# Seventeen tiles of a decoder layer transposed by DMA instead of on TensorE, with modulation in SBUF, earlier residual loads, and the last FFN1 tile normalised in other memory

## The reference

```python
# adaLN: (LayerNorm without affine) * (1 + scale) + shift; shift, scale, gate come from c
h = modulate(x, sh1, sc1)
y = swiglu(h, ffn1_w_gate[l], ffn1_w_up[l], ffn1_w_down[l])
x = layer_norm(ALPHA * x + 0.5 * g1[:, None, :] * y, ln1_g[l], ln1_b[l])
h = modulate(x, sh2, sc2)
y = token_mix(h, w_in[l], attn_sinks[l], pool_w_mix[l], pool_scale[l], w_out[l])
x = layer_norm(ALPHA * x + g2[:, None, :] * y, ln2_g[l], ln2_b[l])
h = modulate(x, sh3, sc3)
y = swiglu(h, ffn2_w_gate[l], ffn2_w_up[l], ffn2_w_down[l])
x = layer_norm(ALPHA * x + 0.5 * g3[:, None, :] * y, ln3_g[l], ln3_b[l])
```

## Time and profile before

| | |
|---|---|
| profiled execution, its own time | 2340.32 us |
| its span (core 1, the slowest) | 2338.8 us; the 8 cores have 2327.7 to 2338.8 us |
| median of three runs | 2362.72 us |
| granted TensorE clock, by core | 0.992 to 0.998 |
| PE, DVE, ACT, POOL busy | 96%, 62%, 33%, 17% of the span |
| data moved | 415.48 MB, mean 178 GB/s |

### The profile page before, as it was taken

The page is one execution under the profiler, slowest core; times in us unless marked ns, Lnnn a source line. Parts: engine busy times, 40 slices in busy tenths (PEclk is TensorE's granted clock), DMA queues, the critical chain, the costliest instruction groups (busy, mean ns, idle before and its releaser), DMA issues.

```text
span 2338.8 us, 41640 instructions; the slowest of 8 cores (2327.7 to 2338.8 us)
## 1 busy us (share of the span) xinstructions
PE 2247.5 (96%) x13832; PEld 1262.8 (54%) x13832; DVE 1447.0 (62%) x2928; ACT 764.9 (33%) x1554; POOL 389.2 (17%) x319
## 2 busy tenths in 40 slices
PE   1998999999999999999999999999999999999998
PEld 1554555555555556644555555555555555555555
DVE  5564465665564343378767676768585858676754
ACT  2521222222222232344343433433343343433321
POOL 0022321221110110013211111111111111211110
PEclk9999999999999999999999999999999999999999
DMA  9973889976563122043645454636464545454556
GB/s 310 312 228 108 164 197 202 202 190 162 181 210 99 70 78 85 1 172 106 242 178 201 162 217 148 231 140 226 154 223 156 208 171 199 177 191 173 208 185 238
DMA packets 123122, 415.48 MB, mean 178 GB/s; under 512 B 27296, under 2 KB 49568, under 8 KB 101408
## 3 DMA queue, kind: packets, MB, share of 16 engines
q1 hardware_dynamic: 87920, 396.92, 49.6%
q0 software_dynamic: 33696, 14.62, 5.4%
q10 hardware_dynamic: 1296, 1.29, 0.2%
HBM read 385.33 MB, written 56.10 MB: 189 GB/s over the span
## 4 chain that ended last, share of the span: by engine, by line
PE 83%; DVE 6%; DMA 5%; issue 3%; SPq 1%; ACT 1%; POOL 1%; DVEq 0%; POOLq 0%; ACTq 0%
PE ps L1239 24%; PE ps L497 23%; PE ps L1262 12%; PE ps L603 8%; PE ps L1046 3%; PE ps L1016 2%; PE ps L1166 2%; PE ps L1168 2%; PE ps L442 2%; DMA t_arena<-x_c 2%; PE ps L578 1%; DMA t_arena<-w_ada_t 1%; SPq L367 1%; DVE t_stt L388 1%; DMA t_arena<-ffn_w_down 1%
## 5 line engine op out<-in xcount | busy, mean ns | idle before, releaser
L497 PE MATMUL ps<-t_arena 128*128 128x384 bf16 x3872 | 638.5, 327 | 21.0 <-ACT t_arena L424 17.9
L1239 PE MATMUL ps<-t_arena 128*128 128x384 bf16 (+1 forms) x3872 | 634.0, 321 | 1.2 <-DVE t_arena L426 1.2
L497 PEld LDWEIGHTS ps<-t_arena 128*128 128x128 bf16 x3872 | 379.2, 98 | 275.9 <-issue 28.6
L1239 PEld LDWEIGHTS ps<-t_arena 128*128 128x128 bf16 x3872 | 371.2, 98 | 243.3 <-issue 20.9
L392 POOL TENSOR_TENSOR t_stt<-t_stt,t_mhalf 128x1 f32<-128x1 f32 x193 | 120.5, 624 | 1437.5 <-DVE t_stt L391 1398.1
L399 ACT ACTIVATE t_arena<-t_arena,t_stt 128x1024 f32<-128x1024 f32 (+1 forms) x193 | 238.9, 1239 | 315.6 <-DVE t_stt L394 291.6
L488 DVE TENSOR_TENSOR t_arena<-ps,t_sg 128x384 bf16<-128x384 f32 x242 | 134.2, 556 | 302.1 <-PE ps L497 293.5
L1262 PE MATMUL ps<-t_arena 128*128 128x512 bf16 x1408 | 314.1, 379 | 2.0 <-DMA t_arena<-scr_d 2.0
L388 DVE BATCH_NORM_STATS2 t_stt<-t_arena 128x6 f32<-128x512 f32 x386 | 266.8, 691 | 51.6 <-DMA t_arena<-x_c 16.8
L603 PE MATMUL ps<-t_arena 128*128 128x512 bf16 x1320 | 292.5, 380 | 5.9 <-DVE t_arena L550 5.2
L527 POOL TENSOR_TENSOR t_arena<-t_arena 128x1024 f32<-128x1024 f32 x95 | 229.1, 2412 | 351.5 <-DVE t_arena L526 338.8
(11 more groups left out here) (90 smaller groups left out, 1513.3 us busy)
## 6 DMA issues: line engine op xcount, KB each, us to landing
t_arena<-scr_gu SPq DMA_DIRECT2D x121, 1024.0 KB, 7.1
t_arena<-scr_d SPq DMA_DIRECT2D x44, 1024.0 KB, 4.9
t_arena<-w_ada_t SPq DMA_DIRECT2D x72, 512.0 KB, 9.2
t_arena<-x_c SPq DMA_DIRECT2D x66, 512.0 KB, 5.8
t_arena<-scr_x SPq DMA_DIRECT2D x65, 512.0 KB, 7.1
t_arena<-ffn_w_gu SPq DMA_DIRECT2D x44, 512.0 KB, 11.5
t_arena<-ffn_w_down SPq DMA_DIRECT2D x44, 512.0 KB, 5.5
scr_x<-t_arena SPq DMA_DIRECT2D x33, 512.0 KB, 3.8
```

The lines of the kernel that those rows point to most:

```text
L497: ins = e.matmul(bk.f[:, 0:T], lhsT=w.ap[:, kc, gu, s2 * 128:(s2 + 1) * 128], rhs=hT.ap[:, kc, 0:T], start=(kc == 0), stop=(kc == 7))
L1239: ins = e.matmul(bk.f[:, 0:T], lhsT=wv[:, kc, gu, s2 * 128:(s2 + 1) * 128], rhs=hTc.ap[:, kc, 0:T], start=(kc == 0), stop=(kc == 7))
```

## The change

There are four edits. (1) `transposes` now has two ways. For FFN1 tiles 2 to 9 and mixer tiles 2 to 10, each block is transposed by one DMA issued by SP, from the `n2` buffer (128x1024 bf16, 256 KB) straight to the `hT` buffer (128x8x128), with one semaphore for all DMAs into a buffer; then the modulation runs in place in SBUF, as eight instructions of 128x384, four on DVE and four on ACT (`modulate`), which wait for the last of the DMAs. The first DMA of a tile waits until the `hT` buffer is free. The tiles 0, 1 and 10 of FFN1, -1, 0 and 1 of the mixer, and all of FFN2 keep the PE way (`pe_transposes`). (2) FFN1's next tile is normalised during the gate/up of the tile before, and its DMAs wait for the end of that gate/up (`tgate`). (3) `prefetch` loads the residual blocks of tiles 2 to 8 during gate/up, as soon as the next tile is normalised. (4) The normalised blocks of tile 10 go to three `n2o` buffers of their own, in the memory of `aTs[1]`, and that tile no longer waits for the transposes of tile 9. Also, mixer tile t (from 2) may be prepared once mixer tile t - 1 is projected and FFN2 tile t - 2 transposed, where it waited for the last gate/up product of FFN2 tile t - 2 before.

```diff
--- before.py
+++ after.py
 -373,6 +373,7 
             def __init__(self, name, lo):
                 self.ap = view(lo, [8, 384])
                 self.bufs = [P.buf(f"{name}_{k}", lo + k * 768, lo + (k + 1) * 768) for k in range(8)]
+                self.sem = P.new_sem("d_" + name)
 
         class AT:
             def __init__(self, name, lo):
 -431,7 +432,7 
             yield from until(*keys)
             ring.give(item)
 
-        def transposes(n2s, hT, mi, tag, prio):
+        def pe_transposes(n2s, hT, mi, tag, prio):
             T = len(n2s) * 128
             for r in range(4):
                 bk = yield from take(XB)
 -447,8 +448,38 
                     S.spawn(hT_evac(bk, 2 * r + j, T, hT, mi, (tag, "ev", 2 * r + j), j, r), 0)
                 S.spawn(free_when(XB, bk, (tag, "ev", 2 * r), (tag, "ev", 2 * r + 1)), 0)
             for n2 in n2s:
+                (n2.ring or NR).give(n2)
+            yield from until(*[(tag, "ev", k) for k in range(8)])
+            flags.add(tag + ("hT",))
+
+        def modulate(T, hT, mi, kc):
+            v = hT.ap[:, kc, 0:T]
+            sc, bi = msc[:, 2 * mi + 1, kc:kc + 1], msc[:, 2 * mi, kc:kc + 1]
+            rd = [hT.bufs[kc], B_msc[2 * mi], B_msc[2 * mi + 1]]
+            if kc % 2:
+                return Op("act", lambda e: e.activation(out=v, in_=v, func=AF.Identity, scale=sc, bias=bi), rd, [hT.bufs[kc]], 0.5, lag=9.0)
+            return Op("dve", lambda e: e.tensor_scalar(out=v, in0=v, scalar1=sc, scalar2=bi, op0=ALU.mult, op1=ALU.add), rd, [hT.bufs[kc]], 0.36, lag=9.0)
+
+        def by_dma(tag):
+            return tag[0] == "t1" and 2 <= tag[1] <= 9 or tag[0] == "t2" and tag[1] >= 2
+
+        def transposes(n2s, hT, mi, tag, prio):
+            T = len(n2s) * 128
+            if not by_dma(tag):
+                yield from pe_transposes(n2s, hT, mi, tag, prio)
+                return
+            for i, n2 in enumerate(n2s):
+                yield Op("sp", lambda e, i=i, n2=n2: e.dma_start_transpose(out=hT.ap[:, :, i * 128:(i + 1) * 128], in_=n2.ap),
+                         [n2.buf], hT.bufs if i == 0 else [], 0.1, hT.sem, 262144)
+            ev = (hT.sem, P.dcnt[hT.sem])
+            for bf in hT.bufs:
+                bf.last_w = ev
+            for n2 in n2s:
+                n2.buf.readers[hT.sem] = ev[1]
                 NR.give(n2)
-            yield from until(*[(tag, "ev", k) for k in range(8)])
+            flags.add((tag[0] + "tr", tag[1]))
+            for kc in range(8):
+                yield modulate(T, hT, mi, kc)
             flags.add(tag + ("hT",))
 
         def load_block(dram, gb, rd=()):
 -465,7 +496,11 
             Ring.gives += 1
             return n2s
 
-        def pre_ffn1(t, hT, gate=()):
+        n2_own = [Tile(f"n2o{i}", A1 + i * 2048, [1024]) for i in range(3)]
+        for n2 in n2_own:
+            n2.ring = Ring([])
+
+        def pre_ffn1(t, hT, gate=(), tgate=(), own=None):
             yield from until("mh", *gate)
             box = [[] for _ in range(3)]
             for i in range(3):
 -473,8 +508,14 
                     S.spawn(mod_block(None, box[i], ("n1", t, i), keep=x_first[3 * t + i], back=True), 2)
                 else:
                     S.spawn(mod_block(load_block(x_c, 3 * t + i), box[i], ("n1", t, i)), 2)
-            n2s = yield from take_n2(3, box)
+            n2s = own or (yield from take_n2(3, box))
+            if own:
+                for b, n2 in zip(box, own):
+                    b.append(n2)
+                Ring.gives += 1
             yield from until(*[("n1", t, i) for i in range(3)])
+            flags.add(("t1ln", t))
+            yield from until(*tgate)
             yield from transposes(n2s, hT, 0, ("t1", t), 2)
 
         wgu = [Tile(f"wgu{j}", G + j * 8192, [8, 2, 256]) for j in range(NGRP)]
 -498,6 +539,16 
                                    start=(kc == 0), stop=(kc == 7))
                 return ins
             return Op("pe", mm, wguq[wgu.index(w)] + hT.bufs, [bk.buf], 8 * mm_n(T))
+
+        pre_res = {}
+
+        def prefetch(t):
+            pre_res[t] = [[] for _ in range(3)]
+            yield from until(("t1ln", 10 if t == 8 else t + 1))
+            for b in range(3):
+                x = yield from take(XR)
+                yield load_block(x_c, 3 * t + b)(x)
+                pre_res[t][b].append(x)
 
         def gateup1(pairs, tag):
             lag = 3 * (len(pairs) - 1)
 -593,8 +644,9 
         def down1(t, aT, tag):
             for b in range(3):
                 gb = 3 * t + b
-                box = []
-                S.spawn(res_load(load_block(x_c, gb), box, XH if t == 10 and b < 2 else XR), 2)
+                box = pre_res[t][b] if t in pre_res else []
+                if t not in pre_res:
+                    S.spawn(res_load(load_block(x_c, gb), box, XH if t == 10 and b < 2 else XR), 2)
                 for h in range(2):
                     bk = yield from take(FB)
                     for part in range(2):
 -874,12 +926,11 
             yield from down1(1, aTs[1], "S0")
             for t in range(2, 9):
                 yield from until(("t1", t, "hT"))
+                S.spawn(pre_ffn1(t + 1, hTs[0], (("x1", 3 * t - 1),), ((("T", t), "gu"),)), 2)
+                if t == 8:
+                    S.spawn(pre_ffn1(10, hTs[1], ("bg", ("t1ln", 9)), own=n2_own), 2)
+                S.spawn(prefetch(t), 3)
                 yield from gateup1([(hTs[0], aTs[0])], ("T", t))
-                if t < 8:
-                    S.spawn(pre_ffn1(t + 1, hTs[0]), 2)
-                else:
-                    S.spawn(pre_ffn1(9, hTs[0]), 2)
-                    S.spawn(pre_ffn1(10, hTs[1], ("bg", ("t1", 9, "hT"))), 2)
                 yield from until((("T", t), "aT", 0, 21))
                 yield from down1(t, aTs[0], ("T", t))
             yield from until(("t1", 9, "hT"), "bg")
 -1299,7 +1350,7 
             S.spawn(m_pre(-1, [0], ()), 2)
             yield from m_proj(-1, [0], 1, False)
             for t in range(NT2):
-                S.spawn(m_pre(t, m_tiles[t], () if t == 0 else ((("S9", "gu"),) if t == 1 else (("C", t - 2, 21),))), 2)
+                S.spawn(m_pre(t, m_tiles[t], () if t == 0 else ((("S9", "gu"),) if t == 1 else (("proj", t - 1), ("t3", t - 2, "hT")))), 2)
                 yield from m_proj(t, m_tiles[t], t % 2, True)
                 for b, gb in enumerate(m_tiles[t]):
                     S.spawn(att_block(t, b, gb, t % 2), 1)
```

## The result

The median of the changed kernel is 2335.55 us over 19 runs, that of the kernel before, on the same chip, 2362.1 us over 19. Some executions of either kernel ran up to 18% longer, with one die or both at a lower granted clock; the medians include them, the ratio leaves them out. It is **0.9938, 95% interval 0.991 to 0.9966**: some 0.6% faster, well inside the 2% that I called no change. The profiled execution took 2335.15 us where 2318 was forecast and 2340.32 was measured before: 5.2 us of the 22.3. Averaged over the eight cores, which is less subject to chance than the slowest one, the span went from 2333.5 to 2322.7 us: 10.8 of 22.3. Both are single executions; 13 executions of the change have a mean span of 2324.5 us, with a standard deviation of 1.6, which makes it 9.0.

A forecast was written before the change was run, and what follows sets the result against it. The prediction took PE, busy 96% of the span, as the bound: 2340.3 us less 22.3 for 400 transposes, all other terms 0, gave 2318 us. Range 2298 to 2368, with 0.85 for a result within 2%.

The forecast's parts named there:

- Part 1: FFN1 and mixer: PE loses 400 of 784 transposes at 0.0558 us each, 22.3 us off.
- Part 2: FFN1 and mixer: 50 transposing DMAs, hidden behind PE's matmuls; cost taken as 0.
- D: Time for a tile's three transposing DMAs in a row; taken near 10 us, between 5.1 and 14.8.
- cover: PE work hiding the DMAs and modulation: 28.5 us of down in FFN1, 15.6 to 18.2 us of gate/up in the mixer.
- The forecast for this step: Sign to look for: 5 to 14 us from the third DMA's issue to the first modulation.
- a little late: Rival, chance 0.17: the three DMAs take 15 to 20 us, outlasting the mixer's cover; 2345 us at 17, 2372 at 20.
- slow transposes: Rival, chance 0.12: each transposing DMA adds 7.7 us, as with 128-byte pieces, and PE waits in the mixer; 2429 us.
- Part 3: Queues of SP, DVE and ACT: loads, stores and products behind the new waits do not delay PE; cost 0.
- Part 4: Moved normalisation and residual loads, tile 10's own memory, modulation in SBUF, mixer order: costed at 0.
- crowded DVE: Rival, chance 0.08: in the stretch with attention PE waits 1 to 3 us for each of 9 tiles; 2327 to 2345 us.
- Waits of PE after 100 us under 25 us: Sign to look for: PE's waits after the first 100 us of the span stay under 25 us in all.

The follow-up runs named there:

- ffn_pe: The change, but with FFN1 tiles 2 to 9 transposed by PE and only the mixer's tiles by DMA; ratio to the kernel before 0.998.
- casts_late: The change, with POOL's casting DMAs begun only behind the gate/up of FFN1 tile 4; ratio to the kernel before 1.0003.
- from6_again: The change, but FFN1's earlier normalisation, residual loads ahead and DMA transposes begin with tile 6, as the casts end; ratio to the kernel before 0.9874.
- no_prefetch: The change without the residual loads ahead, which are at the down again; ratio to the kernel before 0.9928.
- edit1: The DMA transposes alone on the kernel before, with its order of normalisation, residual loads and mixer; ratio to the kernel before 1.0233.

## Why the prediction was right or wrong

**Part 1, the transposes of PE: right, within the scatter.** 384 are left. In the mixer 11.4 us came by ffn_pe where 11.6 were counted, and FFN1's share, 10.7, is there once the residual loads are gone (11.6 by the table, with an uncertainty of some 3).

**Part 2, the transposing DMAs: right in D and its cover, if not free beside the casts.** The queue that SP fills had 87920 packets before and has now:

```profile
q1 hardware_dynamic: 140720, 410.04, 54.6%
```

The 52,800 more are 1056 for each of 50 DMAs: about the 1024 pieces of 256 bytes. They were cheaper than the 0.060 us that I had from the earlier trace rows: the queue's share rose by 5.0 points with them, as an estimate 0.05 x 16 x 2333.6 / 52800 = 0.035 us each, if the queue's other packets took what they took before. D can be seen in two places on core 2, first in FFN1:

```profile
584.17 28.01 PE L655 MATMUL ps<-t_arena 128*128 128x512 bf16 x129
584.41 5.44 SPq L472 DMA_TRANSPOSE t_arena<-t_arena  x3
600.03 2.49 ACT L460 ACTIVATE t_arena<-t_arena,t_msc 128x384 bf16<-128x384 bf16 x4
601.37 3.27 DVE L461 TENSOR_SCALAR t_arena<-t_arena,t_msc 128x384 bf16<-128x384 bf16 x4
```

In FFN1 the first is issued as the down begins, the modulation starts 15.6 us after it and ends 7.5 us before the down does. In the mixer the third DMA is issued by 1397.18 and the modulation begins 7.6 us later, the projection without idle time behind the gate/up:

```profile
1388.59 8.59 SPq L472 DMA_TRANSPOSE t_arena<-t_arena  x3
1390.96 18.36 PE L1290 MATMUL ps<-t_arena 128*128 128x384 bf16 x112 [0.22 <-DVE t_arena L1260]
1404.82 0.37 DVE L461 TENSOR_SCALAR t_arena<-t_arena,t_msc 128x384 bf16<-128x384 bf16 x1
...
1409.15 5.36 PE L1067 MATMUL ps<-t_arena 128*128 128x384 bf16 x32
```

The forecast for this step was 5 to 14 us, and FFN1's is inside it too (589.85 to 600.03, 10.2 us). Over the nine tiles of the mixer and eight cores it is 5.9 to 12.8 us, 8.9 in the median. The cover was smaller than the 15.6 to 18.2 us counted: from the issue of the third DMA to the projection 10.6 to 20.8 us, 13.7 in the median, and on core 2 the modulation is done only 0.1 to 1.1 us before the projection begins. The 976 projection matmuls (L1067, L1076 and L1097 on this core) had 0.8 us of idle time in front of them in all, so "a little late" and "slow transposes" did not happen. The four modulations took 2.5 us on ACT and 3.3 on DVE in FFN1, where 2 was counted; the cover held that too. What Part 2 left out is that three of these DMAs beside the casts hold SP for some 12 us and share the DMA engines with the loads, which is where its 5.6 us of the table may lie; that is argued, not shown.

Of the two pages of the Trainium skill that spoke against each other, the trace sides with Advanced Engine Details and Errata, section X-Bar Transpose (TRN2), that such DMAs are as fast as regular ones: 3.3 us to landing beside 3.6 for a plain one of the same 256 KB (from SBUF to DRAM). The 1309 ns for each 128x128 of VectorE: DVE Perf Modes, section The three transpose paths, may hold for a single one, which no run here shows, but they do not add up: eight in one DMA would be 10.5 us as an estimate.

**Part 3, what waits behind the new waits: right in the main.** The weight loads `scr_gu` of FFN2 still land after 6.8 to 7.0 us (cores 2 and 3; 7.1 in the earlier trace rows), and PE waited for 1.1 us for the `scr_d` ones behind 1000 us (mean of eight cores).

**Part 4, the other edits: here the prediction failed.** It costs the moved normalisation and residual loads at 0, with "PE never waited for them" and "DVE is only 55% busy in FFN1". This term, the cost of the moved steps in FFN1, is the step that failed. Both rows were true and answered another question. The first says that the loads were in time *in the down*, where a late one costs nothing; the edit puts them in front of products that PE needs every 2.6 us. The second is from 540 to 630 us, and a busy share says nothing of an engine that stands still in front of a load. The stretch with casts, where x_c takes 7.8 us in place of 4.5 even before the change, stood in the same trace. In place of 0 the runs give +4.3 for the normalisation and +9.9 for the residual loads beside transposing DMAs (+3.4 without them), some 3.4 of it as a lower clock. The other half of the failure is that I had no rival for FFN1: "crowded DVE" put the same mechanism into the mixer, where L1260 and L1170 cost PE a few microseconds, and the mixer still gained 12.0. That rival's 2327 to 2345 holds the measured 2335.15, and so does my range, but by luck: the waits that came lie in FFN1, where neither had a cost. "Waits of PE after 100 us under 25 us" was wrong twice: they were 30 us even before the change (mean of the cores) and are 41 now, since I had summed only the largest groups of one core.

The rest of the distance to 2318 is the slowest core: it is 10.9 us above the mean of the eight after, and was 5.3 above it before. In part that is chance; but over 13 executions of the change it is 8.7 above on average, and 5.9 over 13 of before, so some 3 us of it stay, and why is open.

## What to carry to other kernels

Before a step that waits for a load is moved, ask what stands behind it on its engine at the new place, and how late that load is in the busiest stretch that it will run in. Rows from one tile do not price an edit that is repeated in all of them: cut the span by what else runs there (casts, background work) and read each part. A DMA transpose was a good trade in this PE-bound kernel where its input was ready a whole phase ahead; without that lead the same instructions made PE wait for 35 us in FFN1 alone.

## What the runs showed of the hardware

- A transposing DMA of 128x1024 bf16 (256 KB) had some 1056 packets, and landed after 3.3 us in a quiet stretch (core 3), 6.4 with FFN2's weight loads (core 2) and 7.6 beside the casts (core 3).
- SP is held longer by it than by a plain load: 5.44 us for three in the quiet down above, 11.58 beside the casts, where most plain loads took 0.33 to 0.5 each. The row is from core 3 of the change; the last two rows show something else, the second of two DVE instructions from SBUF to SBUF (373 ns in the median, up to 2408) stretched beside a POOL instruction:

```profile
301.52 11.58 SPq L472 DMA_TRANSPOSE t_arena<-t_arena  x3
...
320.20 2.69 DVE L461 TENSOR_SCALAR t_arena<-t_arena,t_msc 128x384 bf16<-128x384 bf16 x2
320.43 2.35 POOL L578 TENSOR_TENSOR t_arena<-t_arena 128x1024 f32<-128x1024 f32 x1 [5.08 <-DVE t_arena L577]
```

On each of the eight cores this happens to five of the 68: each of the five starts 0.06 us after a POOL instruction of L578 has begun, ends 0.12 us after it has ended, and takes 2.40 us; on core 3 the one just ahead of it, which starts before that of L578, takes 0.37. What the two share was not tried by itself.
- PE's waits went with a lower clock: with 10.1 us more of them in 240, the granted clock of 280 to 520 us fell from 0.998 to 0.983, as an estimate another 3.4 us. In casts_late, without waits, it is 1.00 and in from6_again, with 2.9 us, too; in no_prefetch, with 6.2, it is 0.99, and in edit1, with 18.0, 0.97.
